# Down projection of a ConvFFN layer: the latent tokens as seven block products of 512 tokens, 1408 features and 512 columns, the context tile beside them

## The chip, the cores and the metric

The kernel runs on one core of a Trainium2 chip, in float32 with each operand split into a high part that the matmul takes exactly (float32r) and a low remainder. The metric is the device time of one execution in microseconds (us).

## The reference, cut to what matters

One trunk layer of a hybrid diffusion backbone. 128 context tokens and 1024 latent tokens (1152 in all, 9 tiles of 128) share the weights; only the gates (`gt2`) differ. The last steps are what the change touches:

```
up = dwconv_rows(h2 @ w_up, conv_w, conv_b);  ug, uv = split(up)
f  = (gelu(ug) * uv) @ w_down            # (1152 x 2816) @ (2816 x 1024)
x  = x + gt2 * rmsnorm(f, g_post_ffn)    # root mean square over all 1024 columns
```

## The kernel before, in words

The features (2816 = 22 tiles of 128) come out of the up projection transposed, features on partitions, and go to a DRAM scratch `f_dram`. The up projection itself already runs as seven block products per feature tile pair; ScalarE (ACT) makes the high parts, VectorE (DVE) the low parts and the sums out of PSUM, GpSimd (POOL) the sums of weight blocks (`weight_sum`, L902) and the product of gate and value (L915).

The down projection follows it. Its work is cut into 66 cells (`down_cell`): for each of three rounds r of 384 tokens, 22 feature tiles k. A cell needs 128 x 1024 weights and 128 x 384 features. They are loaded by SyncE (SP) into one of four slots (`down_load`, `f_load`; a cell's load waits until the cell four earlier is ready), ACT copies both to their high parts (`down_split` in ACT, L1822 and L1824), DVE subtracts to get the low parts (`down_split` in DVE, `sub_hi`, L1927) and signals `down_ready`. TensorE (PE) then runs 18 matmuls of 512 columns (3 token tiles x 2 column halves x 3 products high*high, high*low, low*high; L1326). PE's `down_used` or `done2` frees the slot for ACT.

A round's three tiles of 1024 columns are in three of four pairs of PSUM banks. After its last cell, ACT squares each tile out of PSUM with a running sum (`final_stats`), DVE makes mean, reciprocal root and the product with the gate row into `yo` (`finish`, L2508), POOL adds the residual `x1ld` (L941) and issues the stores and the next loads of the residual. The last tile is finished by DVE alone and stored by SP and ACT, half by half; the last four cells run tile by tile (`down_end`).

The order on each engine is written out by hand; all waits are semaphores. In the last unit of the up projection (s = NP-1), `next_weights` puts the splits of cells 0 to 2 among the taps and sums of that unit on ACT and DVE; cell 3's split comes after the unit's last gelu and taps.

Of the kernel before, what the change touches and what calls it, by code (L numbers as in the profile page):

```python
# [27 lines left out]
P = 128  # L28
# [79 lines left out]
def build(nc, x_prompt, x_sample, state_C, state_n, state_m, c, c_ctx, w_ada, b_ada, g_pre_mix, g_post_mix,  # L108
# [197 lines left out]
    for n, name in enumerate(quarters):  # L306
# [26 lines left out]
    down_at = [R + 32 * HT + 16 * n * HT for n in range(DR)]  # L333
    down_hi = [place(f"down_hi{n}", [P, 1024], F32R, at=at) for n, at in enumerate(down_at)]
    down_lo = [place(f"down_lo{n}", [P, 1024], F32R, at=at + 4096) for n, at in enumerate(down_at)]
    down_raw = [place(f"down_raw{n}", [P, 1024], at=at + 4096 * h)
                for n, (at, h) in enumerate((raw_at[(NP + b) % 2], h) for b in range(2) for h in range(2))]
    f_hi = [place(f"f_hi{n}", [P, BW], F32R, at=HH0 + 4 * T * n) for n in range(DR)]
    f_lo = [place(f"f_lo{n}", [P, BW], F32R, at=HH0 + 32 * T + 4 * T * n) for n in range(DR)]
    g_at = [LD0 + 8192 + 4 * T] + [HH0 + 4 * T * (4 + n) for n in range(1, DR)]  # L340
    f_raw = [place(f"f_raw{n}", [P, BW], at=at) for n, at in enumerate(g_at)]
    x1ld = place("x1ld", [P, 4, DM], at=R)
    yo = place("yo", [P, 3, DM], at=R + 96 * HT)
    y_junk = place("y_junk", [P, DM], at=R + 96 * HT + 12288)
# [19 lines left out]
    plain_g_dram = nc.dram_tensor("z_plain_g", (PLAIN, P, T), F32, kind="Internal").ap()  # L364
    f_dram = nc.dram_tensor("z_f", (NF, P, T), F32, kind="Internal").ap()
# [66 lines left out]
    x1_in = [S(f"x1_in{i}") for i in range(4)]  # L432
    last_done = S("last_done")
    y_stored = [S("y_stored0"), S("y_stored1"), S("y_stored2")]
    y_last = [S("y_last0"), S("y_last1")]
# [29 lines left out]

    def put_out(eng, t):

        if t < NT - 1:
            eng.wait_ge(final_done, t + 1)
        else:  # L470
            eng.wait_ge(last_done, 1)
            eng.dma_start(y_sample[0, (t - 1) * P:t * P, 0:512], yo[:, t % 3, 0:512]).then_inc(y_last[1], 16)
            return
        dst = y_prompt[0] if t == 0 else y_sample[0, (t - 1) * P:t * P, :]
        eng.dma_start(dst, yo[:, t % 3, :]).then_inc(y_stored[t % 3] if t < NT - 2 else y_last[t - NT + 2], 16)

# [55 lines left out]

    def down_cell(n):
        return n % NF, n // NF

    def down_slot_free(eng, n):

        k, r = down_cell(n - DR)
        if k == NF - 1:
            eng.wait_ge(done2, NT + TB * (r + 1))  # L540
        else:
            eng.wait_ge(down_used, n - DR - r + 1)
# [56 lines left out]
    with nc.Block() as block:  # L599

        @block.sync
        def _(sp):
# [108 lines left out]
            def down_load(n):  # L711

                k, r = down_cell(n)
                if n < DR:
                    sp.wait_ge(up_lo_done, 7 * (NP - 1 + n // 2))
                else:
                    sp.wait_ge(down_ready, n - DR + 1)
                sp.dma_start(down_raw[n % DR][:, :], w_down[0][k * P:(k + 1) * P, :]).then_inc(down_in[n % DR], 16)

            def f_load(n):  # L720

                k, r = down_cell(n)
                if n == 0:
                    sp.wait_ge(plain_stored, 16 * 3 * PLAIN)
                elif n < DR:
                    sp.wait_ge(product_done, 7 * (NP - 1) + 2)
                if r == 0 and k >= PLAIN:
                    for half in range(2):
                        sp.wait_ge(half_stored[half], 16 * (k - PLAIN + 1))
                sp.dma_start(f_raw[n % DR][:, :], f_dram[k][:, r * BW:(r + 1) * BW]).then_inc(f_in[n % DR], 16)  # L730
# [8 lines left out]
            for s in range(NP):  # L739
                if s + 2 < NP:  # L740
                    sp.wait_ge(up_lo_done, 7 * (s + 1))
                    up_load(s + 2)
                elif s == NP - 2:
                    down_load(0)
                    down_load(1)
                    f_load(0)
                else:
                    down_load(2)
                    down_load(3)
# [7 lines left out]
                if s == NP - 1:  # L757
                    for n in range(1, DR):
                        f_load(n)
            for n in (DR, DR + 1):  # L760
                down_load(n)
                f_load(n)
            half_store(NP - 1, 0)
            half_store(NP - 1, 1)
            for n in range(DR + 2, NB * NF):
                down_load(n)
                f_load(n)
            put_out(sp, NT - 2)
            put_out(sp, NT - 1)

            for d in range(3):
                sp.wait_ge(y_stored[d], 16 * ((NT - d) // 3))
            sp.wait_ge(y_last[0], 16)
            sp.wait_ge(y_last[1], 32)
# [5 lines left out]
        def _(pool):  # L780
# [154 lines left out]
            pool.wait_ge(product_done, 7 * (NP - 1) + 5)  # L935
            for t in range(4):
                pool.dma_start(x1ld[:, t % 4, :], x1_dram[t]).then_inc(x1_in[t % 4], 16)
            for t in range(NT - 1):
                pool.wait_ge(evac2, NT + t + 1)
                pool.wait_ge(x1_in[t % 4], 16 * (t // 4 + 1))  # L940
                pool.tensor_tensor(yo[:, t % 3, :], yo[:, t % 3, :], x1ld[:, t % 4, :], ALU.add).then_inc(final_done, 1)  # L941
                if t < NT - 2:
                    put_out(pool, t)
                if t + 4 < NT:
                    pool.wait_ge(final_done, t + 1)
                    pool.dma_start(x1ld[:, t % 4, :], x1_dram[t + 4]).then_inc(x1_in[t % 4], 16)


        @block.tensor
        def _(pe):  # L950
# [362 lines left out]
            def down_tile(n, j, halves=(0, 1)):  # L1313

                k, r = down_cell(n)
                q = TB * r + j
                bank = SLOT_BANK[(7 * NP + q) % 4]
                if k == 0 and halves[0] == 0:
                    if q >= 4:
                        pe.wait_ge(evac2, NT + q - 3)  # L1320
                    else:
                        product_freed(pe, 7 * NP - 4 + q)
                tok = slice(j * P, (j + 1) * P)
                for x, w, first, last in ((f_hi, down_hi, True, False), (f_hi, down_lo, False, False), (f_lo, down_hi, False, True)):
                    for hb in halves:
                        mm = pe.matmul(ps[:, bank + hb, :], x[n % DR][:, tok], w[n % DR][:, hb * 512:(hb + 1) * 512],  # L1326
                                       start=(k == 0 and first), stop=(k == NF - 1 and last))
                return mm

            def down_feature(n):  # L1330

                k, r = down_cell(n)
                pe.wait_ge(down_ready, n + 1)
                for j in range(TB):
                    mm = down_tile(n, j)
                    if k == NF - 1:
                        mm.then_inc(done2, 1)
                if k < NF - 1:
                    mm.then_inc(down_used, 1)

            def down_end():

                for j in range(TB - 1):
                    for n in range(NB * NF - DR, NB * NF):
                        if j == 0:
                            pe.wait_ge(down_ready, n + 1)
                        mm = down_tile(n, j)
                    mm.then_inc(done2, 1)
                for n in range(NB * NF - DR, NB * NF):
                    mm = down_tile(n, TB - 1, (0,))  # L1350
                mm.then_inc(done1, 1)
                for n in range(NB * NF - DR, NB * NF):
                    mm = down_tile(n, TB - 1, (1,))
# [32 lines left out]
            for n in range(NB * NF - DR):  # L1386
                down_feature(n)
# [4 lines left out]
        def _(act):  # L1392
# [420 lines left out]
            def down_split(n):  # L1813

                k, r = down_cell(n)
                d = n % DR
                act.wait_ge(down_in[d], 16 * (n // DR + 1))
# [4 lines left out]
                act.activation(down_hi[d][:, :], down_raw[d][:, :], ACT.Copy)  # L1822
                act.wait_ge(f_in[d], 16 * (n // DR + 1))
                act.activation(f_hi[d][:, :], f_raw[d][:, :], ACT.Copy).then_inc(down_hi_done, 1)  # L1824

            def next_weights(s, i):
# [3 lines left out]
                elif i in (2, 3, 4):  # L1830
                    down_split(i - 2)
# [50 lines left out]
            def final_stats(q):  # L1882

                bank = SLOT_BANK[(7 * NP + q) % 4]
                if q == NT - 1:

                    act.wait_ge(done1, 3 * KD + NB * PLAIN + 1)
                    act.wait_ge(final_roots, 2 * q)
                    act.activation(y_junk[:, 0:512], ps[:, bank, :], ACT.Square, accum_out=hstat[:, 0, q:q + 1]).then_inc(final_roots, 1)
# [657 lines left out]
```

## Time and profile before

| what | us |
|---|---|
| median of 3 runs (1790.91 to 1791.72) | 1791.66 |
| the profiled execution | 1790.54 |
| its span, first to last instruction | 1788.7 |
| PE busy, DVE busy, ACT busy, POOL busy in the span | 1771.9, 1128.6, 672.3, 283.2 |
| down projection: first to last start of its matmuls | 1508.1 to 1778.6 |
| its 1188 matmuls, mean duration of one | 0.39 |

The profile's page gives, for one execution, each engine's busy time, the busy share in slices of the span, the DMA queues, the chain that ended last, and groups of like instructions with their mean duration and the wait ahead of them. A matmul's duration overlaps the next one's: the pace is read from starts. The mean granted TensorE clock is 0.998 of full speed.

### The profile page before, as it was taken

What the parts mean: (1) busy time and instruction counts of PE and PEld (TensorE: products, weight loads), DVE (VectorE), ACT (ScalarE), POOL (GpSimd) and SP (SyncE); (2) the same over time, 40 slices, a digit from 0 to 9 for tenths busy, and PEclk for the clock granted to TensorE, in tenths of its full rate; (3) what the DMA queues carried; (4) which work ended last, traced back from release to release, by engine and by line L of the source; (5) the groups of instructions that cost most, each with busy time, mean ns of one, the idle gap of its engine ahead of it and who ended that gap; (6) DMA issues with size and microseconds to landing.
All of it is one profiled execution on the core that took longest, in us unless ns stands there. A gap on an engine that the chain in (4) does not pass through costs nothing.

```text
span 1788.7 us, 26788 instructions
## 1 busy us (share of the span) xinstructions
PE 1771.9 (99%) x10627; PEld 1659.0 (93%) x10627; DVE 1128.6 (63%) x2330; ACT 672.3 (38%) x1132; POOL 283.2 (16%) x278
## 2 busy tenths in 40 slices
PE   9999999999999999999999999999999999999997
PEld 3999999999999999999988999999999999888886
DVE  4786566565566544463555688888888888454543
ACT  3723212333134243451344544443444444343432
POOL 1010000100000100010010252444333333020101
PEclk9999999999999999999999999999999999999999
DMA  9133334424433544373332322333222223757562
GB/s 349 51 98 113 93 102 128 126 76 152 105 115 126 148 116 143 131 253 110 97 123 86 112 95 81 107 113 99 84 75 71 81 79 115 271 185 241 182 225 76
DMA packets 200720, 229.66 MB, mean 128 GB/s; under 512 B 9840, under 2 KB 163324, under 8 KB 200596
## 3 DMA queue, kind: packets, MB, share of 16 engines
q1 hardware_dynamic: 183060, 164.66, 30.3%
q0 software_dynamic: 13056, 46.39, 7.5%
q10 hardware_dynamic: 4480, 16.91, 2.3%
q8 instruction: 84, 1.38, 0.3%
q14 instruction: 40, 0.33, 0.1%
HBM read 180.77 MB, written 47.15 MB: 127 GB/s over the span
## 4 chain that ended last, share of the span: by engine, by line
PE 91%; DVE 5%; SPq 1%; ACT 1%; issue 1%; DMA 1%; DVEq 0%; ACTq 0%
PE ps L1298 22%; PE ps L1326 14%; PE ps L958 12%; PE ps L960 12%; PE ps L959 12%; PE ps L1240 5%; PE ps L1123 2%; PE ps L1124 2%; PE ps L1125 2%; PE ps L1107 2%; PE ps L1111 2%; PE ps L1109 2%; DVE ada_part L2146 1%; DVE H_lo L1927 1%; PE ps L987 1%
## 5 line engine op out<-in xcount | busy, mean ns | idle before, releaser
L958 PE MATMUL ps<-H_hi,ring_hi 128*128 128x384 f32 x1224 | 422.6, 345 | 0.9 <-DVE H_lo L1927 0.4
L959 PE MATMUL ps<-H_lo,ring_hi 128*128 128x384 f32 x1224 | 409.5, 335 | 0.0
L960 PE MATMUL ps<-H_hi,ring_lo 128*128 128x384 f32 x1224 | 409.5, 335 | 0.0
L958 PEld LDWEIGHTS ps<-H_hi,ring_hi 128*128 128x128 f32 x1224 | 229.9, 188 | 4.2 <-DVE H_lo L1927 2.1
L959 PEld LDWEIGHTS ps<-H_lo,ring_hi 128*128 128x128 f32 x1224 | 230.1, 188 | 1.0
L960 PEld LDWEIGHTS ps<-H_hi,ring_lo 128*128 128x128 f32 x1224 | 229.8, 188 | 0.0
L1927 DVE TENSOR_TENSOR down_lo<-down_raw,down_hi 128x1024 fp32r<-128x1024 f32 x66 | 86.0, 1303 | 122.9 <-ACT f_hi L1824 122.6
L2110 DVE SCALAR_TENSOR_TENSOR Cst<-Cst,GE,ps 128x257 f32<-128x257 f32 x56 | 27.0, 483 | 165.4 <-PE ps L1111 165.4
L1298 PE MATMUL ps<-T_hi,up_hi 128*128 128x288 f32 x608 | 130.5, 296 | 0.4 <-ACT held_g L1803 0.3
L1298 PE MATMUL ps<-T_hi,up_lo 128*128 128x288 f32 x608 | 130.2, 296 | 0.0
L1298 PE MATMUL ps<-T_lo,up_hi 128*128 128x288 f32 x608 | 130.1, 296 | 0.0
L1927 DVE TENSOR_TENSOR up_lo<-up_raw,up_hi 128x512 fp32r<-128x512 f32 x114 | 88.4, 779 | 57.5 <-ACT up_hi L1761 57.5
L1326 PE MATMUL ps<-down_hi,f_hi 128*128 128x512 f32 x396 | 122.9, 390 | 0.5 <-DVE yo L2508 0.5
L1326 PE MATMUL ps<-down_lo,f_hi 128*128 128x512 f32 x396 | 122.6, 389 | 0.0
L1326 PE MATMUL ps<-down_hi,f_lo 128*128 128x512 f32 x396 | 122.6, 389 | 0.0
L1822 ACT ACTIVATE down_hi<-down_raw 128x1024 fp32r<-128x1024 f32 x66 | 69.9, 1059 | 140.2 <-PE ps L1326 125.2
L2146 DVE SCALAR_TENSOR_TENSOR ada_part<-raw,condT,ada_part 128x128 f32<-128x128 f32 x448 | 120.3, 346 | 0.0
L1927 DVE TENSOR_TENSOR ring_lo<-raw,ring_hi 128x1024 fp32r<-128x1024 f32 (+1 forms) x69 | 82.4, 1198 | 33.1 <-ACT ring_hi L1410 30.2
L1298 PEld LDWEIGHTS ps<-T_hi,up_hi 128*128 128x128 f32 x608 | 97.8, 189 | 1.3 <-ACT held_g L1803 0.9
L561 ACT ACTIVATE stage<-ps 128x384 f32<-128x384 f32 x72 | 35.2, 488 | 168.5 <-PE ps L960 168.5
L1298 PEld LDWEIGHTS ps<-T_lo,up_hi 128*128 128x128 f32 x608 | 97.9, 189 | 0.0
L1298 PEld LDWEIGHTS ps<-T_hi,up_lo 128*128 128x128 f32 x608 | 97.9, 189 | 0.0
(298 smaller groups left out, 3578.2 us busy)
## 6 DMA issues: line engine op xcount, KB each, us to landing
down_raw<-in_w_down_dram SPq DMA_DIRECT2D x66, 512.0 KB, 3.7
raw<-in_w_in_dram SPq DMA_DIRECT2D x44, 512.0 KB, 4.1
up_raw<-in_w_up_dram SPq DMA_DIRECT2D x38, 512.0 KB, 5.2
raw<-in_w_ada_dram SPq DMA_DIRECT2D x32, 512.0 KB, 5.4
f_raw<-z_f SPq DMA_DIRECT2D x66, 192.0 KB, 3.8
GE<-z_gates SPq DMA_DIRECT2D x72, 128.0 KB, 4.1
z_f<-mid_v SPq DMA_DIRECT2D x19, 288.0 KB, 5.2
z_f<-mid_g SPq DMA_DIRECT2D x19, 288.0 KB, 2.1
```

The costliest lines, as they stand in the source:

```text
L958: pe.matmul(out, whi, xhi, start=first, stop=False)
L959: pe.matmul(out, whi, xlo, start=False, stop=False)
L960: return pe.matmul(out, wlo, xhi, start=False, stop=last)
L1107: pe.matmul(ps[:, 5 + d, 0:VW], Pt[:, d, :], vaug[v][:, cx, :], start=True, stop=(i == 0))
L1109: mm = pe.matmul(ps[:, 5 + d, 0:VW], qs[:, d, :], Cst[:, d, :], start=False, stop=True)
L1111: mm = pe.matmul(ps[:, 7, 0:VW], k_weighted[:, d, :], vaug[v][:, cx, :], start=True, stop=True)
L1240: mm = pe.matmul(ps[:, bank + hb, :], x[:, k, tok], w[:, hb * 512:(hb + 1) * 512], start=(n == 0 and first), stop=(n == KD - 1 and last))
L1298: mm = pe.matmul(ps[:, bank + sb, 0:SB], wt[:, w], x[:, k0 + k, cols], start=(k == 0 and n == 0), stop=(k == KD // 2 - 1 and n == 2))
L1326: mm = pe.matmul(ps[:, bank + hb, :], x[n % DR][:, tok], w[n % DR][:, hb * 512:(hb + 1) * 512], start=(k == 0 and first), stop=(k == NF - ...
L1822: act.activation(down_hi[d][:, :], down_raw[d][:, :], ACT.Copy)
L1927: return dve.tensor_tensor(out, full, hi.bitcast(F32), ALU.subtract)
L2146: ins = dve.scalar_tensor_tensor(out=part, in0=w, scalar=condT[:, cond, k:k + 1], in1=part, op0=ALU.mult, op1=ALU.add)
```

## The change

The three rounds are replaced by seven products over the latent tokens. With X11, X12 the two feature halves (11 tiles each) of the first 512 latent tokens, X21, X22 those of the second 512, and W11 to W22 the quarters of `w_down` (1408 features x 512 columns), the products are formed from sums and differences of blocks on both sides, and the four result quarters (`c11`, `c12`, `c21`, `c22`, in SBUF) from sums of products. A cell is now one feature tile of one product: 77 cells, n = 11 p + j. PE runs 12 matmuls in a cell (4 token tiles x 3), and 15 in products 0, 2 and 6, in which the context tile's 128 tokens go along (`down_context`). The context's last block, kept back in `fk_hi`, `fk_lo`, `W12_hi`, `W12_lo`, runs after everything else (33 matmuls). PSUM: products alternate between two sets of four banks.

What each engine does per cell after: SP loads a 128 x 512 weight block, in products 1, 3, 4 and 5 a second one; POOL subtracts the two there (and stores the difference in products 3 and 4, to be read in 4 and 5); ACT copies weight and feature tile to high parts (128 x 512 each, 128 x 128 more with the context); DVE subtracts for the low parts, and makes the feature combination (`combine`) in products 1 to 4. At a product's end ACT (product 0) or DVE (`product_sums`) takes the four banks out of PSUM. Statistics are taken by halves; POOL adds the residual and issues a store for each 128 x 512 half tile of the latent tokens.

The diff, cut to what sets the order and the work:

```diff
 # ---- SP
+                if n >= DR:
                     sp.wait_ge(down_ready, n - DR + 1)
+                    if (n - DR) // NC in (3, 4):
+                        m = diff_no(n - DR) - NC
+                        sp.wait_ge(w_diff_stored[m % 2], 16 * (m // 2 + 1))
...
+                sp.dma_start(w_raw[d][:, :], first).then_inc(down_in[d], 16)
+                if p in DIFF:
...
+                    sp.dma_start(w_sub[d][:, :], second).then_inc(down_in[d], 16)
...
                 elif s == NP - 2:
-                    down_load(0)
-                    down_load(1)
-                    f_load(0)
+                    for n in range(DR):
+                        w_load(n)
...
                 if s == NP - 1:
-                    for n in range(1, DR):
+                    for n in range(DR):
                         f_load(n)
...
+                if n == 6 * NC + DR - 1:
+                    for i in range(4):
+                        x1_load(i)
+            sp.wait_ge(down_ready, CELLS)
+            for i in range(4, NT):
+                x1_load(i)
 # ---- POOL
-                pool.tensor_tensor(yo[:, t % 3, :], yo[:, t % 3, :], x1ld[:, t % 4, :], ALU.add).then_inc(final_done, 1)
+            for p in DIFF:
+                for j in range(NC):
...
+                    pool.tensor_tensor(w_raw[d][:, :], w_raw[d][:, :], w_sub[d][:, :], ALU.subtract).then_inc(weight_sums, 1)
+                    if p in (3, 4):
...
+                        pool.dma_start(w_diff_dram[p - 3][j], w_raw[d][:, :]).then_inc(w_diff_stored[m % 2], 16)
+            for i, t in enumerate(X1_ORDER[:NT - 1]):
+                pool.wait_ge(x1_in[i % 3], 16 * (i // 3 + 1))
+                for h in range(2):
+                    c = slice(512 * h, 512 * (h + 1))
+                    pool.wait_ge(last_done, 2 * i + h + 1)
+                    pool.tensor_tensor(half_tile(t, h), half_tile(t, h), x1t[t][:, c], ALU.add).then_inc(final_done, 1)
+                    pool.wait_ge(final_done, 2 * i + h + 1)
+                    pool.dma_start(y_sample[0, (t - 1) * P:t * P, c], half_tile(t, h)).then_inc(y_stored, 16)
 # ---- PE
+                if j == 0:
+                    product_freed(pe, 7 * NP - 2) if p == 0 else pe.wait_ge(evac2, summed_at[p - 1, 0])
...
+                tail = range(CELLS - TAIL_CELLS, CELLS)
+                for t in TILE_ORDER:
+                    for n in tail:
+                        if t == TILE_ORDER[0]:
                             pe.wait_ge(down_ready, n + 1)
+                        mm = down_tile(n, t)
                     mm.then_inc(done2, 1)
+                for n in tail:
+                    down_context(n)
+                pe.wait_ge(evac2, summed_at[6, TILE_ORDER[0]])
+                for j in range(NC):
+                    mm = down_mm(SET[1][0], fk_hi[j][:, :], fk_lo[j][:, :], W12_hi[j][:, :], W12_lo[j][:, :], False, j == NC - 1)
 # ---- ACT
+                act.activation(B_hi[d][:, :], w_raw[d][:, :], ACT.Copy)
+                if p in (0, 2) or cell_inputs(n):
+                    act.wait_ge(f_in[d], f_count(n))
+                if p in (1, 3, 4, 6):
+                    act.wait_ge(combined, NC * {1: 0, 3: 1, 4: 2, 6: 3}[p] + j + 1)
...
+                ins = act.activation(A_hi[d][:, :], src[:, :], ACT.Copy)
...
-                elif i in (2, 3, 4):
-                    down_split(i - 2)
+                elif i in (3, 4, 5):
+                    down_split(i - 3)
...
+            for n in range(3, CELLS):
+                if n == last_cell(0) + DR:
+                    first_copies()
+                if n == last_cell(2) + DR + 2:
+                    for t in (1, 2, 3, 4, 0):
+                        half_squares(t)
...
+                if n == last_cell(5) + DR + 4:
+                    for t in (5, 6, 7, 8):
+                        root(t)
                 down_split(n)
 # ---- DVE
+                if n + 1 < CELLS and (n + 1) // NC == 1:
+                    combine(n + 1)
+                if p in (2, 3, 4):
+                    combine(n)
                 dve.wait_ge(down_hi_done, n + 1)
+                sub_hi(B_lo[d][:, :], w_raw[d][:, :], B_hi[d][:, :])
...
+                ins = sub_hi(A_lo[d][:, :], src[:, :], A_hi[d][:, :])
...
+                    elif p == 3:
+                        steps = ((c22, c21, ALU.add), (c12, c12, ALU.add))
+                    elif p == 4:
+                        steps = ((c21, c21, ALU.add), (c22, c22, ALU.add), (c12, c12, ALU.add))
...
+                    for out, x, op in steps:
+                        ins = dve.tensor_tensor(out[:, t, :], x[:, t, :], q, op)
...
+            for n in range(3, CELLS):
+                for p in range(1, 6):
+                    if n == last_cell(p) + DR:
+                        product_sums(p)
...
+                if n == last_cell(5) + DR + 5:
+                    for t in (5, 6, 7, 8):
+                        gated(t)
                 down_split(n)
+            product_sums(6)
+            for t in LAST_TILES:
+                mean(t)
+                gated(t)
```

`gated(t)` takes a reciprocal and two in-place products of a half tile in SBUF with the gate row in SBUF (128 x 512 each).

## Rows read from the trace of the kernel before

**Rows 1.** The chain that ended last, from 1480 us: start, us, what.
```profile
1479.87 28.38 PE ps L1298 x213
1508.25 85.70 PE ps L1326 x378
...
1691.65 87.35 PE ps L1326 x384
```
**Rows 2.** Engines' busy time in the down projection: stretch, us, busy and instructions.
```profile
1508.00:1778.70 270.70, 270.17 (x1190) 222.62 (x1189) 136.83 (x162) 107.25 (x156) 30.84 (x26) 1.00 0.58 194
```
**Rows 3.** DVE's timeline in the middle of a round: start, us, engine, line, operation.
```profile
1641.39 1.23 DVE L1927 TENSOR_TENSOR down_lo<-down_raw,down_hi 128x1024 fp32r<-128x1024 f32 x1 [2.39 <-ACT f_hi L1824]
...
1645.47 1.23 DVE L1927 TENSOR_TENSOR down_lo<-down_raw,down_hi 128x1024 fp32r<-128x1024 f32 x1 [2.39 <-ACT f_hi L1824]
```
**Rows 4.** Groups of one tile or line: duration ns min/median/max, first and last start.
```profile
L1927 DVE TENSOR_TENSOR up_lo<-up_raw,up_hi x114: 678/686/1782, 1067.0 to 1492.4; 128x512 fp32r<-128x512 f32 x114
L902 POOL TENSOR_TENSOR up_raw<-up_raw x38: 1287/1296/1698, 1056.8 to 1483.5; 128x512 f32<-128x512 f32 x38
L941 POOL TENSOR_TENSOR yo<-yo,x1ld x8: 2382/2406/2415, 1599.6 to 1776.7; 128x1024 f32<-128x1024 f32 x8
L2485 DVE TENSOR_TENSOR yo<-ps,gtb x2: 683/686/690, 1777.1 to 1779.9; 128x512 f32<-128x512 f32 x2
```
**Rows 5.** Timeline of DVE, ACT and POOL in the up projection's seven-product stage.
```profile
1400.22 0.75 DVE L2387 TENSOR_TENSOR held_v<-held_v,ps 128x576 f32<-128x576 f32 x1
1400.48 1.30 POOL L902 TENSOR_TENSOR up_s<-up_raw 128x512 f32<-128x512 f32 x1 [4.30 <-DVE up_lo L1927]
1401.08 0.76 DVE L2387 TENSOR_TENSOR held_g<-held_g,ps 128x576 f32<-128x576 f32 x1
...
1403.74 0.69 DVE L1927 TENSOR_TENSOR up_lo<-up_raw,up_hi 128x512 fp32r<-128x512 f32 x1
1403.97 1.74 POOL L915 TENSOR_TENSOR mid_v<-mid_g,mid_v 128x576 f32<-128x576 f32 x1 [2.20 <-DVE mid_v L2401]
1404.34 2.82 DVE L2401 SCALAR_TENSOR_TENSOR mid_g<-held_g,vT,mid_g 128x567 f32<-128x567 f32 x2
```
**Rows 6.** Timeline after the first round: PE's gap, DVE's subtraction, POOL's add and issue.
```profile
1599.59 0.73 PE L1326 MATMUL ps<-down_hi,f_hi 128*128 128x512 f32 x2 [0.21 <-DVE yo L2508]
...
1603.08 3.86 DVE L1927 TENSOR_TENSOR down_lo<-down_raw,down_hi 128x1024 fp32r<-128x1024 f32 x1
1603.43 2.42 POOL L941 TENSOR_TENSOR yo<-yo,x1ld 128x1024 f32<-128x1024 f32 x1
1606.15 0.58 POOL L475 DMA_DIRECT2D out_dram<-yo  x1 [0.30 <-POOL yo L941]
```
**Rows 7.** Timelines of ACT, SP and DVE where the down projection begins.
```profile
1482.71 0.68 DVE L1927 TENSOR_TENSOR up_lo<-up_raw,up_hi 128x512 fp32r<-128x512 f32 x1
1483.31 0.75 DVE L2387 TENSOR_TENSOR held_v<-held_g,ps 128x576 f32<-128x576 f32 x1
...
1486.59 0.62 ACT L1761 ACTIVATE up_hi<-up_raw 128x512 fp32r<-128x512 f32 x1
...
1499.07 1.41 SPq L730 DMA_DIRECT2D f_raw<-z_f  x3
...
1501.63 0.53 ACT L1824 ACTIVATE f_hi<-f_raw 128x384 fp32r<-128x384 f32 x1 [1.42 <-DMA f_raw<-z_f]
...
1509.36 0.75 DVE L2387 TENSOR_TENSOR held_v<-held_v,ps 128x576 f32<-128x576 f32 x1
...
1517.77 1.23 DVE L1927 TENSOR_TENSOR down_lo<-down_raw,down_hi 128x1024 fp32r<-128x1024 f32 x1 [2.19 <-ACT f_hi L1824]
```
**Rows 8.** DMA issues from 1500 us to the end: KB each, median us to landing.
```profile
down_raw<-in_w_down_dram SPq DMA_DIRECT2D x62, 512.0 KB, 3.7
f_raw<-z_f SPq DMA_DIRECT2D x64, 192.0 KB, 3.8
```
**Rows 9.** DMA issues from 1514 to 1530 us, and the engines' row of 1515 to 1530 (last two columns: DMA share, GB/s).
```profile
down_raw<-in_w_down_dram SPq DMA_DIRECT2D x5, 512.0 KB, 10.4
...
1515.00:1530.00 15.00, 15.00 (x68) 12.43 (x67) 7.18 (x9) 6.48 (x10) 3.55 (x5) 1.00 0.80 299
```
**Rows 10.** The end: PE's last piece of the chain, then ACT's square and last store.
```profile
1775.81 3.19 PE ps L1326 x14
...
1779.02 0.60 ACT L1891 ACTIVATE y_junk<-ps 128x512 f32<-128x512 f32 x1 [2.03 <-PE ps L1326]
1779.51 0.19 ACT L1891 ACTIVATION_READ_ACCUMULATOR y_junk<-ps 128x1 f32 x1
...
1782.13 0.34 ACTq L1896 DMA_DIRECT2D out_dram<-yo  x1
```

More of the change, by code:

```diff
@@ L339, in build @@
[L339 to L344, printed above, removed]
+    h_piece = lambda g, k, half: HH0 + 32 * T * g + 4 * T * k + 4 * HT * half
+    X11 = [place(f"X11_{j}", [P, 512], at=h_piece(j // KD, j % KD, 0)) for j in range(NC)]
@@ new lines, in f_count, with w_count, diff_no, w_diff_count @@
+    def f_count(n):
+        return 16 * sum(cell_inputs(m) for m in range(n % DR, n + 1, DR))
+    def w_count(n):
+        return 16 * sum(2 if m // NC in DIFF else 1 for m in range(n % DR, n + 1, DR))
+    def diff_no(n):
+        p, j = down_cell(n)
+        return NC * DIFF[p] + j
+    def w_diff_count(n):
+        return 4 * NP + diff_no(n) + 1
+    done_at, at = {}, NT
+    for p in range(7):
+        for t in TILE_ORDER:
+            at += 1
+            done_at[p, t] = at
+        if p in (0, 2):
+            at += 1
+            done_at[p, "c"] = at
@@ new lines, in build @@
+    done_at[6, "c"] = at + 1
+    summed_at, at = {}, NT
+    for p in range(1, 7):
+        for t in TILE_ORDER + (("c",) if p == 2 else ()):
+            at += 1
+            summed_at[p, t] = at
+    last_cell = lambda p: NC * (p + 1) - 1
+    LAST_TILES = tuple(t + 1 for t in TILE_ORDER)
+    stat_of, root_of, mean_of = {}, {}, {}
+    for n, (what, t) in enumerate([("half", t) for t in (1, 2, 3, 4, 0, 5, 6, 7, 8)] + [("rest", t) for t in (5, 6, 7, 8)]
+                                  + [("root", t) for t in (5, 6, 7, 8)]
+                                  + [(what, t) for t in LAST_TILES + (0,) for what in ("rest", "root")]):
+        (root_of if what == "root" else stat_of)[what, t] = n + 1
@@ L536, in down_slot_free, with half_tile @@
+    for n, (what, t) in enumerate([("half", t) for t in (1, 2, 3, 4, 0, 5, 6, 7, 8)] + [("rest", t) for t in (5, 6, 7, 8)]
+                                  + [("rest", t) for t in LAST_TILES + (0,)]):
+        mean_of[what, t] = n + 1
+    X1_ORDER = (5, 6, 7, 8) + LAST_TILES + (0,)
+    def half_tile(t, h):
+        if t == 0:
+            return c0[h][:, :]
+        return ((c11, c12) if t < 5 else (c21, c22))[h][:, (t - 1) % 4, :]
     def down_slot_free(eng, n):
-        k, r = down_cell(n - DR)
@@ L727, in f_load @@
-                if r == 0 and k >= PLAIN:
+                elif n == NC:
+                    sp.wait_ge(product_done, 7 * NP)
+                if (p == 0 and k >= PLAIN) or p == 2:
                     for half in range(2):
                         sp.wait_ge(half_stored[half], 16 * (k - PLAIN + 1))
-                sp.dma_start(f_raw[n % DR][:, :], f_dram[k][:, r * BW:(r + 1) * BW]).then_inc(f_in[n % DR], 16)
+                elif n == NC:
+                    for half in range(2):
+                        sp.wait_ge(half_stored[half], 16 * NP)
@@ L1311, in up_pair @@
                 product(s, 6, H_hi, H_lo, KD // 2, HT)
[L1313 to L1328, printed above, removed]
@@ new lines, in sum_squares, with half_squares @@
+            def sum_squares(what, t, src, sums):
+                n = stat_of[what, t]
+                if n > 1:
+                    act.wait_ge(final_roots, n - 1)
+                act.activation(y_junk[:, :], src, ACT.Square, accum_out=sums[:, 0, t:t + 1]).then_inc(final_roots, 1)
+            def half_squares(t):
+                act.wait_ge(evac2, summed_at[2, "c" if t == 0 else t - 1] if t < 5 else summed_at[4, t - 5])
+                sum_squares("half", t, half_tile(t, 0 if t < 5 else 1), hstat)
```

410 lines of the change are left out of this document (261 added, 149 removed).

## The prediction

> **What bounds the kernel now.** I read the chain that ended last first: from 1480 us it is PE alone but for short pieces between rounds [rows 1], so the down projection is bound by matmuls. Then the busy times there: PE 270.2 of 270.7 us, DVE 136.8, ACT 107.3, POOL 30.8 [rows 2]. Then the pace: DVE's splits of one cell begin 4.08 us apart, each after a wait of 2.4 us [rows 3], which is 18 matmuls at 0.2267 us. Last, pairs of overlapping instructions on DVE and POOL, because the change gives both more work per matmul.
>
> **What PE saves.** Before: 66 x 18 = 1188 matmuls. After: 77 x 12 = 924 for the latent tokens, and 4 x 33 = 132 for the context, 1056 in all. 132 x 0.2267 = 29.9 us. If every edit had cover, the span would be about 1759.
>
> **What DVE and POOL do to each other.** A POOL subtraction of 128x512 takes 1.29 us, DVE's 0.686 [rows 4]; in a row DVE starts one 0.60 after another (1482.71 to 1483.31 [rows 7]). When both inputs of the DVE instruction are in SBUF, the two take turns: a low-part subtraction of 1.23 us took 3.86 while POOL added for 2.42 [rows 6]; POOL's product at 1403.97 took 1.74 behind a DVE subtraction, and the DVE pair after it 2.82 [rows 5]. When one DVE input is in PSUM, neither is longer (0.75 and 0.76 beside 1.30 [rows 5]). So a POOL subtraction costs up to 1.29 us of DVE's time, except under PSUM sums and while DVE waits anyway. Before, eight adds lay in 270 us; now there are 44 subtractions and 16 half adds.
>
> **Cell by cell.** PE needs 12 x 0.2267 = 2.72 us for a cell, 3.40 with the context. DVE needs:
> - Products 0 and 6: two low parts and a 128-column one, 1.5 us (2.1 with W12's): covered.
> - Product 1: combination and two low parts 1.83, POOL 1.29, so 3.12. It loses 0.4 a cell over seven cells after the boundary; the lead there is about 4 us (three ready cells, 8.2, less ACT's last copy 0.6, two ACT copies 1.2, low parts 1.3, POOL 1.3). Hidden.
> - Product 2: 2.1 of 3.4, no POOL but at its end. Hidden.
> - Products 3 and 4: DVE combines (0.69), waits for ACT's copy of the result (0.62 [rows 7] and the semaphores), then subtracts twice (1.25): 2.6 us in series, and nothing of it overlaps the cell before, since `combine(n)` is issued only just ahead of its own wait. POOL adds between 0.65 (it fits into DVE's wait) and 1.29. Weights land about 4 us after their issue [rows 8], the wait falls at no fixed phase of that, so I take 0.85: 3.45 a cell against 2.72.
> - Product 5: 1.22 + 1.29 = 2.5. Just covered.
>
> **The middle.** From the end of product 2 to the start of product 5's fourth cell PE needs 25 cells x 2.72 = 68.0 us. DVE, which has nothing beyond three ready cells, needs: five sums of product 2, 3.1 (0.62 each, from 0.686 [rows 4]); 19 cells x 3.45 = 65.5; five means and one product 1.2; the wait for ACT's five squares (0.6 + 0.19 each [rows 10]), of which about 2.0 is not hidden; eight sums of product 3, 5.0; three cells of product 5, 7.5; twelve sums of product 4, 7.4; one more split, 1.3. Sum 93.0; POOL gets about four subtractions done under the PSUM sums, -5.0: 88. **PE stalls 20 us.** Bounds: with no turns taken at all 73.3 us, a stall of 5; with every POOL subtraction added in full 101.6, a stall of 34.
>
> **The start.** Features of cell 0 are now loaded only after the half store at 1498.7, where three loads went before at 1499.07, and ACT waited until 1501.63 for one of them [rows 7]. Now it is two per cell, and ACT's and DVE's split of cell 0 stands ahead of the last unit's sums; PE's context matmuls wait for the sum that ran at 1509.36. That sum comes some 3 us later, and cell 3 (1517.77 + 1.6 before [rows 7]) at about 1521.5, where PE's three cells last 10.2 us instead of 12.2. I take 3.5 us; bounds 1 (only the shorter cells) and 6.
>
> **Transfers.** Products 1, 3 and 4 move 768 KB in 2.72 us, 289 GB/s, against 172 before. A stretch of 15 us at 299 GB/s had the DMA engines busy 0.80 [rows 9], so it fits, and the ring gives 10.9 us for load (5), POOL (1.3), two copies (1.2) and low parts (1.3). Cost 0 to 10, taken as 0. In product 6 SP issues four residual loads of 512 KB in a row and stops at the fourth until the first has landed; when such four were under way before, weights took 10.4 us [rows 9]. With ACT's four squares, roots and table load I take 3 us for products 5 and 6 (0 to 8).
>
> **The tail.** Before cell 74, DVE gates four tiles (8 instructions of 0.65, both inputs in SBUF), and POOL follows with 8 adds of 1.29 with 0.3 + 0.58 for wait and DMA issue between them [rows 6]. DVE starts this about 4.2 us after cell 69's matmuls end, and its work to cell 76's readiness is 5.2 + 0.8 (reciprocals) + 5.5 (splits), with all of POOL's 10.3 between: 4.2 + 21 = 25 us. PE is there after four cells and two thirds of a tile, 15 us, since the tile order asks for cell 76 almost at once. Stall 9.5; bounds 1 (no turns) and 15 (PE has no lead by then).
> From T, when cell 76 is ready, PE has 72 matmuls, 16.3 us, and the context's own end, as long as that from 1779.0 to 1788.7, 9.7 us: T + 26. But POOL ends later. The sums are done at T + 7.5, the first half is gated at T + 9, and eight POOL steps of 2.3 follow, the last add ending at T + 26.4; from the issue of the last store to the end it took 6.6 us [rows 10], and a POOL-issued store a little more: **T + 33.5**, 7.5 behind the context.
>
> **Sum.** Start 1508.2; 984 matmuls up to T, 223.1; stalls 3.5 + 20 + 3 + 9.5 = 36: T = 1767.3. Span 1800.8. The profiled execution was 1.8 over its span, 1802.6; the median of the runs is 1.1 above it: **1803.7**, 12 us or 0.7% slower. The seven products save 30 us of matmuls, and about 42 come back.
>
> The granted clock is 1.00 in the down projection [rows 2], whose gaps on PE are like the 0.21 us ahead of 1599.59 [rows 6], so no row shows it after 9 us of idling. The Trainium skill (TensorE: Matmul & The Clock Gate, What's actually happening) says that an engine that has been idle falls to half rate until it is busy again. By it the four tiles after T would come at half pace, at most 6.8 us later, and POOL's chain with them: about 1810. No run here shows it yet.
>
> **Rivals.**
> - *The cover holds, faster.* One mechanism: POOL's 128x512 work falls into DVE's waits and PSUM sums instead of between subtractions, and decides from the point where a product-3 cell takes DVE under 2.72 us. Then the middle stalls 5, the tail 1, the rest 4.5: T = 1741.8, and with POOL's own end, which stays, a span of 1775.3, **1778**. For it: DVE has a wait of 0.65 per cell and 15 us of PSUM sums, 28 us of room for 28 us of subtractions. Against it: nothing aligns them. Chance 0.27; between it and the forecast, 1788 to 1795, 0.11.
> - *Forecast*, DVE bound in products 3 and 4 and POOL last: 1795 to 1814, 0.47.
> - *Transfers are late as well.* At the 194 GB/s that the stage moved on average [rows 2], 768 KB would take 4.0 us: 33 cells lose 1.2, 41 us in place of the middle's 20: 1825. Speaks for it the ring of only four cells; against, the 299 GB/s. Chance 0.08, and 0.07 for the clock (1810).
>
> **Numbers.** A difference under 0.2% (3.6 us) is about what a measurement of this kernel can't tell from none. Faster 0.28, same 0.10, slower 0.62. Range 1775 to 1817; the likeliest case alone 1795 to 1814.
>
> **What would show it.** PE waiting for DVE (A_lo) in products 3 and 4, about 0.7 us a cell; DVE's subtractions above 0.69 on average there; a PE gap of some 10 us before cell 76; POOL's add and store as the last work, several us after PE's end. It is wrong if products 3 to 5 run at 2.72 us a cell.

## The result, and the profile after

The changed kernel takes 1803.94 us (median of 4 runs, 1802.34 to 1806.74) against 1791.58: a ratio of 1.0071, 95% interval 1.0054 to 1.0089, so 0.7% slower. The forecast was 1803.7. Its profiled execution has a span of 1800.5 us.

The chain that ended last, from the page (shares of the span by engine), had been PE 91% and DVE 5%. Now DVE and POOL stand in it:

```profile
PE 68%; DVE 17%; POOL 4%; issue 4%; ACT 4%; DMA 2%; SPq 1%; DVEq 0%; POOLq 0%; ACTq 0%
```

Busy time by stretch (us; PE, PEld, DVE, ACT, POOL, granted clock, DMA share, GB/s) answers to [rows 2]. The down projection and the places where PE stood still: its start, the sums after products 3 and 4, the wait for cell 76:

```profile
1508.00:1518.00 10.00, 7.52 (x27) 5.81 (x27) 9.71 (x17) 3.84 (x6) 1.47 (x1) 0.83 0.34 106
1649.00:1667.00 18.00, 14.09 (x52) 10.91 (x51) 18.00 (x27) 5.76 (x10) 9.46 (x10) 0.83 0.70 234
1686.00:1702.00 16.00, 13.33 (x53) 10.51 (x52) 12.32 (x21) 8.43 (x18) 6.45 (x6) 0.89 0.43 148
1748.00:1763.00 15.00, 4.70 (x13) 2.52 (x11) 14.96 (x16) 0.00 (x0) 9.36 (x11) 0.67 0.27 105
...
1508.00:1781.00 273.00, 252.04 (x1059) 203.53 (x1058) 219.95 (x324) 117.53 (x243) 106.19 (x91) 0.95 0.65 219
```

In three of them DVE has hardly an idle moment and PE has, and the granted clock falls behind each gap. The groups of like instructions (count | busy us, mean ns | wait before) show who gets longer, against medians of 0.686 and 1.296 us before [rows 4]:

```profile
L1049 POOL TENSOR_TENSOR w_raw<-w_raw,w_sub 128x512 f32<-128x512 f32 x44 | 69.6, 1583 | 99.0 <-DMA w_sub<-in_w_down_dram 90.5 <-DMA w_sub<-z_w_diff 8.3
L2103 DVE TENSOR_TENSOR B_lo<-w_raw,B_hi 128x512 fp32r<-128x512 f32 x77 | 67.3, 874 | 45.4 <-ACT fc_hi L1976 18.2 <-ACT A_hi L1972 16.0 <-ACT fk_hi L1976 11.1
L2103 DVE TENSOR_TENSOR A_lo<-X,A_hi 128x512 fp32r<-128x512 f32 x77 | 63.8, 828 | 0.0
...
L2723 DVE SCALAR_TENSOR_TENSOR c<-c,stat,gtb 128x512 f32<-128x512 f32 x16 | 23.6, 1515 | 0.3
L2702 DVE TENSOR_TENSOR c<-c,ps 128x512 f32<-128x512 f32 x36 | 22.3, 681 | 6.3 <-PE ps L1434 6.3
```

The sums out of PSUM (L2702) keep their 0.68; the means of the groups with two inputs in SBUF are longer. The medians are not (0.69 for the low parts): in the stages with POOL's 44 subtractions, 28 DVE instructions took 1.2 to 2.25 us and the others what they take alone. The 28 come to 28 us more, and POOL's 44 to 13 us more than 1.29 each.

DVE's two bursts of sums, after products 3 and 4, begin shortly before PE's two gaps in the middle (1657.7 and 1694.5):

```profile
1654.18 4.86 DVE L2702 TENSOR_TENSOR c<-c,ps 128x512 f32<-128x512 f32 x8
...
1689.03 7.26 DVE L2702 TENSOR_TENSOR c<-c,ps 128x512 f32<-128x512 f32 x12
```

All terms of the sum. The losses are the distances between the first matmuls of successive cells, less 2.72 or 3.40 us; T is the end of cell 76's split (1762.9):

| term of the sum | forecast | measured |
|---|---|---|
| cells 0 and 1 | 3.5 | 4.4 |
| products 3 to 5 | 20 | 13.6 |
| other boundaries of products, loads | 3 | 1.2 |
| wait for cell 76 | 9.5 | 12.4 |
| T | 1767.3 | 1762.9 |
| from T to the end | 33.5 | 37.6 |
| span | 1800.8 | 1800.5 |

That the total is right to 0.3 us is luck: T came 4.4 us earlier than forecast, and the rest took 4.1 us more. Within T, 6.4 us too much for the middle and 1.8 for the loads stand against 3.8 too little for the start and for cell 76.

### The profile page after: what moved, and what is told of

Same layout as the page of the kernel before. It is cut to its first block, busy times and chain, and to the rows that moved or that the text cites. A ratio compares the mean times of both kernels' runs of the same rounds, so it can differ in the third digit from the quotient of the medians.

```text
span 1800.5 us, 27040 instructions
## 1 busy us (share of the span) xinstructions
PE 1752.6 (97%) x10495; PEld 1639.4 (91%) x10495; DVE 1216.9 (68%) x2493; ACT 680.4 (38%) x1219; POOL 367.6 (20%) x352
## 4 chain that ended last, share of the span: by engine, by line
PE 68%; DVE 17%; POOL 4%; issue 4%; ACT 4%; DMA 2%; SPq 1%; DVEq 0%; POOLq 0%; ACTq 0%
PE ps L1075 12%; PE ps L1077 12%; PE ps L1076 12%; PE ps L1415 8%; PE ps L1357 5%; DVE mid_g L2577 3%; DVE up_lo L2103 3%; DVE mid_v L2577 2%; PE ps L1432 2%; PE ps L1240 2%; PE ps L1433 2%; PE ps L1434 2%; PE ps L1241 2%; PE ps L1242 2%; POOL w_raw L1049 2%
## 5 line engine op out<-in xcount | busy, mean ns | idle before, releaser
L1432 PE MATMUL ps<-B_hi,A_hi 128*128 128x512 f32 x308 | 124.8, 405 | 17.9 <-DVE fc_lo L2103 10.3
L1433 PE MATMUL ps<-B_lo,A_hi 128*128 128x512 f32 x308 | 123.3, 400 | 0.0
L1434 PE MATMUL ps<-B_hi,A_lo 128*128 128x512 f32 x308 | 122.9, 399 | 0.0
L2103 DVE TENSOR_TENSOR B_lo<-w_raw,B_hi 128x512 fp32r<-128x512 f32 x77 | 67.3, 874 | 45.4 <-ACT fc_hi L1976 18.2
L1415 PE MATMUL ps<-H_hi,up_lo 128*128 128x288 f32 x456 | 97.8, 296 | 0.0
```

The lines of the kernel that those rows point to most:

```text
L1415: mm = pe.matmul(ps[:, bank + sb, 0:SB], wt[:, w], x[:, k0 + k, cols], start=(k == 0 and n == 0), stop=(k == KD // 2 - 1 and n == 2))
L1432: pe.matmul(out, xhi, whi, start=first, stop=False)
L1433: pe.matmul(out, xhi, wlo, start=False, stop=False)
L1434: return pe.matmul(out, xlo, whi, start=False, stop=last)
L2103: return dve.tensor_tensor(out, full, hi.bitcast(F32), ALU.subtract)
```

## Experiments

Theory A: DVE instructions with two inputs in SBUF and POOL's 128x512 operations take turns, and that is what PE waits for. Rivals: DVE's bursts of sums (B), the lower clock (C), the transfers (D). "Before" had 1790.6 to 1791.2 us beside these runs.

**e1, the subtraction on POOL left out.**
```diff
-                    pool.tensor_tensor(w_raw[d][:, :], w_raw[d][:, :], w_sub[d][:, :], ALU.subtract).then_inc(weight_sums, 1)
```


> The 44 weight subtractions on GpSimd are left out (the loads and the stores of the blocks stay, so the products use unsubtracted weights). Theory A, VectorE and GpSimd take turns at SBUF: the PE waits in products 3 to 5 (13.6 us, some 4 of them from the lower clock that followed) shrink to 2 or less, VectorE's low-part subtractions there all take 0.69, the gap before cell 76 stays about 12; time 1790 to 1793. Rival B, VectorE's own bursts of 8 and 12 sums are what PE waits for: the waits after products 3 and 4 stay 8 us or more, time 1798 to 1802. Rival D, the transfers are late: nothing changes, 1803.


ACT waits for the load in its place. Measured 1789.5 us (ratio to before 0.9989, 0.9979 to 0.9998). PE lost 1.0 us in products 3 to 5 in place of 13.6, with all bursts of sums and all loads still there. Busy times of the stretch of products 3 to 5 (columns as above), where POOL has nothing but the issues of stores:
```profile
1618.00:1706.00 88.00, 87.59 (x385) 71.94 (x384) 67.73 (x119) 44.84 (x87) 9.18 (x17) 1.00 0.75 244
```
At 244 GB/s and with the bursts PE runs through: B and D fall as causes by themselves. The wait for cell 76 stayed at 12. What e1 can't separate is the turns from the time that ACT waits for POOL's result, as both went.

**e12, a memset in its place.** 128x512 on POOL as before, but only written.
```diff
-                    pool.tensor_tensor(w_raw[d][:, :], w_raw[d][:, :], w_sub[d][:, :], ALU.subtract).then_inc(weight_sums, 1)
+                    pool.memset(w_sub[d][:, :], 0.0).then_inc(weight_sums, 1)
```


> The GpSimd subtraction is replaced by a memset of the second block (128x512, GpSimd only writes; the products use unsubtracted weights). If what is shared is the way in which the second input is read, VectorE's low parts in products 1, 3, 4, 5 take 0.69 as with nothing there, PE's waits stay under 2 us in products 3 to 5 and the time is that of e1, 1790. If any GpSimd access holds VectorE up: means of 0.8 or more and waits of 5 us or more.


A single run: 1789.57 us, 0.9 us lost in products 3 to 5. POOL's line (duration ns min/median/max):
```profile
L1049 POOL MEMSET w_sub<- x44: 525/527/531, 1536.8 to 1697.4; 128x512 f32 x44
```
36 of the 44 overlap a DVE instruction, and no DVE instruction of 128x512 beside them is over 0.8 us: the mean of the low parts is 0.709 and 0.703 as in e1 (0.710, 0.704). So POOL writing does not hold DVE up. ACT waits for POOL here as in the changed kernel, though for 0.53 us of work and not 1.29; a read-free instruction of 1.29 us was not tried.

**e5, the subtraction on DVE**, one cell ahead; the stores stay on POOL.
```diff
-                    pool.tensor_tensor(w_raw[d][:, :], w_raw[d][:, :], w_sub[d][:, :], ALU.subtract).then_inc(weight_sums, 1)
+                if n + 1 < CELLS and (n + 1) // NC in DIFF:    # in DVE's down_split(n)
+                    e = (n + 1) % DR
+                    dve.wait_ge(down_in[e], w_count(n + 1))
+                    dve.tensor_tensor(w_raw[e][:, :], w_raw[e][:, :], w_sub[e][:, :], ALU.subtract).then_inc(weight_sums, 1)
```


> The 44 weight subtractions move from GpSimd to VectorE, one cell ahead; the stores of the differences stay on GpSimd. Theory A (turns at SBUF): a subtraction beside VectorE's work cost it 1.1 us and kept GpSimd waiting up to 4.5 us, on VectorE it costs 0.6 in order; the waits of PE in products 3 to 5 go from 13.6 to 2 to 5 us, the gap before cell 76 stays 12; 1792 to 1796. Rival (VectorE has too much work of any kind): 0.6 us more per cell on VectorE makes it no better, 1803 or more.


Measured 1798.29 us (1.0045, 1.0030 to 1.0060), slower than forecast: products 3 to 5 lose 8.3, not 2 to 5. All 44 subtractions took 0.68 to 0.70 us there, so no turns were taken, and yet two stops of PE stay behind the bursts, 2.0 and 2.2 us. DVE needs 2.4 us for a cell now instead of 1.8 and has less to spare against PE's 2.72; 3.4 of the 8.3 is matmuls at the lower clock. So B is no cause alone, but a partner: DVE's bursts hurt once its work per cell comes near PE's 2.72. The start was worse too (5.9 for 4.4), which no theory here explains.

**e11, only the bursts spread**, one token tile a cell over four cells (the squares and means that follow product 4's sums come two cells later for it).
```diff
+                    if p in (3, 4):
+                        if 0 <= n - last_cell(p) - DR < 4:
+                            product_sums(p, TILE_ORDER[n - last_cell(p) - DR:][:1])
```


> The changed kernel with only the sums of products 3 and 4 spread over four cells each, GpSimd's subtractions kept. If the bursts alone make the 13.6 us of waits in products 3 to 5, they go to 3 or less and the time to 1792. If bursts and turns add up to more than VectorE has, about half stays: waits 4 to 9 us, 1796 to 1800.


Measured 1801.24 us (1.0061, 1.0045 to 1.0078); products 3 to 5 still lose 11.6, where 4 to 9 were expected. With POOL's subtractions in place, how the sums are laid out hardly matters. Bursts and turns make the 13.6 us together: without the turns 1.0 is left (e1), with the turns and without bursts 11.6.

**e2, gates of tiles 5 to 8 behind the last split** (order only: the loop over `gated` moves from before cell 74's split to after `product_sums(6)`).
```diff
-                if n == last_cell(5) + DR + 5:
-                    for t in (5, 6, 7, 8):
-                        gated(t)
                 down_split(n)
             product_sums(6)
+            for t in (5, 6, 7, 8):
+                gated(t)
```


> Order only: the gating of the four tiles 5 to 8 goes behind the last split and product 6's sums. A: no gap before cell 76 (PE gets there at about 1750.5 and not 1762.9), clock stays at full there, but GpSimd then has 16 adds in a row of about 2.2 us after the sums, so the end comes about T + 45 to 50: 1797 to 1803, no gain in time. Rival (cells 74 to 76 are late for their loads or ScalarE): the gap stays 8 us or more.


Measured 1805.36 us (1.0076, 1.0061 to 1.0091), above the 1797 to 1803 expected. The gap is gone, the clock is full there, and the end comes 36 us after PE's last matmul:
```profile
1745.00:1766.00 21.00, 21.00 (x94) 17.40 (x93) 14.53 (x20) 2.08 (x5) 6.43 (x7) 1.00 0.41 150
1766.00:1800.00 34.00, 0.46 (x2) 0.02 (x1) 27.15 (x25) 3.87 (x13) 24.01 (x26) 0.58 0.32 124
```
PE's last matmul came 15 us sooner and the end 2 us later: the 16 adds and gates, in a row, are the path here.

**e4, the adds left out** (no residual in the latent output).
```diff
-                    pool.tensor_tensor(half_tile(t, h), half_tile(t, h), x1t[t][:, c], ALU.add).then_inc(final_done, 1)
-                    pool.wait_ge(final_done, 2 * i + h + 1)
```


> The 16 residual adds on GpSimd are left out (the residual is missing from the latent output; gates and stores stay). A: gates take 0.67 to 0.75 each, the gap before cell 76 goes to 1 us or less, the clock doesn't fall there, and the end is bound by the context's matmuls again, T + 26 to 28: 1779 to 1783. Rival B (VectorE's own eight gates and the tile-by-tile tail are too much): the gap stays 5 us or more, time 1788 or more.


Measured 1782.01 us (0.9950, 0.9933 to 0.9966). Each gate takes what it takes alone, the stores still being issued by POOL:
```profile
L2721 DVE SCALAR_TENSOR_TENSOR c<-c,stat,gtb x16: 743/749/753, 1740.0 to 1766.4; 128x512 f32<-128x512 f32 x16
```
The wait for cell 76 is 0.9 us, and the end comes 25 us after T. Products 3 to 5 lose 14.1 as before. With the adds, the kernel takes 22 us more.

**e3, stores issued by SP** and not between POOL's adds.
```diff
-                    pool.wait_ge(final_done, 2 * i + h + 1)
-                    pool.dma_start(y_sample[0, (t - 1) * P:t * P, c], half_tile(t, h)).then_inc(y_stored, 16)
+                    sp.wait_ge(final_done, 2 * i + h + 1)    # in a loop at SP's end
+                    sp.dma_start(y_sample[0, (t - 1) * P:t * P, c], half_tile(t, h)).then_inc(y_stored, 16)
```


> The 16 output stores of the latent tokens are issued by SyncE at its end and not by GpSimd between its adds. If the DMA issue on GpSimd holds VectorE up as the add does (VectorE's gated halves took 2.2 us, 0.4 more than beside a subtraction alone), a step falls from 2.16 to about 1.95 in the gap before cell 76 and after it: gap 10 to 11 and the end some 2 to 3 us nearer to T, 1799 to 1801. If the issue only uses GpSimd's own time and VectorE is slowed by the add alone: VectorE's gates fall to 1.8, the same sum. If neither: 1804.


Measured 1793.83 us (1.0012, 1.0003 to 1.0022), a gain of 10 us where 3 to 5 were expected: T comes 3.6 us sooner, and the end 30.1 after T and not 37.6. Of these 7.5 us, 5.4 are gone by the end of POOL's last add and 2.1 behind it. POOL's adds run without a break, and DVE's gates fit between them one for one (POOL's line, then DVE's):
```profile
1742.69 8.50 POOL L1067 TENSOR_TENSOR c<-c,x1t 128x512 f32<-128x512 f32 x5
```
```profile
1745.09 3.29 DVE L2726 SCALAR_TENSOR_TENSOR c<-c,stat,gtb 128x512 f32<-128x512 f32 x2
```
That is 1.65 us a gate. In the changed kernel it was 2.1, and DVE's instruction began inside POOL's DMA issue, ahead of the add:
```profile
1745.89 4.21 DVE L2723 SCALAR_TENSOR_TENSOR c<-c,stat,gtb 128x512 f32<-128x512 f32 x2
...
1754.29 2.21 DVE L2103 TENSOR_TENSOR B_lo<-w_raw,B_hi 128x512 fp32r<-128x512 f32 x1
1756.42 2.21 DVE L2103 TENSOR_TENSOR A_lo<-X,A_hi 128x512 fp32r<-128x512 f32 x1
```
```profile
1754.10 0.55 POOL L1064 DMA_DIRECT2D out_dram<-c  x1 [0.30 <-POOL c L1062]
1754.67 1.27 POOL L1062 TENSOR_TENSOR c<-c,x1t 128x512 f32<-128x512 f32 x1
1756.24 0.55 POOL L1064 DMA_DIRECT2D out_dram<-c  x1 [0.30 <-POOL c L1062]
```
DVE's 1754.29 has nothing beside it but the issue for 0.4 us and still ends 0.56 after the add at 1754.67. In e5, where POOL issues stores with no such operation behind them, DVE's subtractions keep 0.69. So the issue alone doesn't hold DVE; an add that stands right behind it seems to do so already then. That is read from these three kernels; which part of POOL takes the turn was not measured.

**e7, PE kept busy in its gap** with 44 matmuls into a free bank.
```diff
+                pe.wait_ge(evac2, summed_at[5, TILE_ORDER[-1]])
+                for m in range(44):
+                    pe.matmul(ps[:, SET[1][1], :], fk_hi[0][:, :], W12_hi[0][:, :], start=True, stop=True)
```


> Added: 44 matmuls of 512 columns (10 us at 0.227) into a free PSUM bank between cell 73 and the wait for cell 74, where PE stood for 10 us and the granted clock fell for 13.7 us. Theory C (the lower clock costs time of its own): matmuls run 0.227 and not 0.427 from cell 76 on, the tiles' sums come 1.7 to 2 us sooner after cell 76 is ready, and the time is 1801 to 1802.5. Rival: GpSimd's chain sets the end and absorbs that, 1804. T itself stays at 1762.9.


Measured 1803.60 us (1.0070, 1.0053 to 1.0086): no gain. The clock is full in the stretch of the gap (the last but two columns), where it was 0.64 in the changed kernel:
```profile
1749.00:1763.00 14.00, 13.43 (x59) 10.81 (x58) 13.96 (x13) 0.51 (x2) 9.85 (x12) 1.00 0.29 112
```
T was 1764.7, as the wait behind product 4's sums was 4.7 us in this execution and not 2.8 (no run here says why), and from T to the end it took 37.5 again. The clock in the tail costs nothing, as the end goes by gates and adds. This run can't price the clock elsewhere: there, the cells behind the gaps (1, 47 and 58) lose 1.3, 2.6 and 1.7 us in the changed kernel, nearly all of it in matmuls 0.43 apart for 0.23: 5.6 us together.

**e6, features first:** the loads of cells 0 to 3 go ahead of the two half stores.
```diff
+                if s == NP - 1:
+                    for n in range(DR):
+                        f_load(n)
                 if s:
                     half_store(s - 1, 0)
                     half_store(s - 1, 1)
```


> Order on SyncE only: the feature loads of cells 0 to 3 go ahead of the two half stores of the last up unit but one. If cell 0's split on ScalarE and VectorE waits for its features and holds the sum that PE's first context matmul waits for, the 4.4 us lost in cells 0 and 1 (3.0 of waiting and 1.4 of the lower clock behind it) fall to 1 to 2 and the time to 1800 to 1802. If VectorE's splits are simply more work ahead of that sum, nothing changes: 1804.


Measured 1798.96 us (1.0043, 1.0028 to 1.0058). The start loses 0.1 us in place of 4.4, where 1 to 2 were expected to stay:
```profile
1508.00:1518.00 10.00, 10.00 (x48) 8.43 (x48) 7.68 (x12) 4.38 (x8) 3.29 (x2) 1.00 0.19 68
```

**e9, all of it on DVE.** e5 and e6, and: the differences are stored by ACT's queue, outputs by SP, and the adds go away. A half is multiplied by the gate row as soon as its squares are taken, and scale and residual are one instruction.
```diff
-                    pool.tensor_tensor(half_tile(t, h), half_tile(t, h), x1t[t][:, c], ALU.add).then_inc(final_done, 1)
+                dve.tensor_tensor(half_tile(t, h), half_tile(t, h), gtb2[:, 1, 512 * h:512 * (h + 1)], ALU.mult)
...
+                    dve.scalar_tensor_tensor(out=half_tile(t, h), in0=half_tile(t, h), scalar=stat[:, 3, t:t + 1],
+                                             in1=x1t[t][:, 512 * h:512 * (h + 1)], op0=ALU.mult, op1=ALU.add).then_inc(last_done, 1)
```


> GpSimd does nothing in the down projection: VectorE subtracts the weights, multiplies by the gate row ahead of the statistics where it can and adds the residual in the same instruction as the scale; differences are stored by ScalarE's queue, outputs by SyncE's; features of the first cells are loaded early. A: waits of PE 2 to 5 us in all, no gap before cell 76, clock full, and PE's context matmuls with their 10 us end set the time: 1508.2 + 239.4 + 4 + 10 = 1762, with what lies around the span 1762 to 1769, faster than both kernels. Rival (the VectorE is overloaded without GpSimd): 1785 or more.


Measured 1766.28 us, ratio to before 0.9865 (0.9850 to 0.9879): 1.35% faster than before, 2.1% faster than the change. DVE does more instructions in less time than in the changed kernel (211.1 us for 220.0), and POOL 3.3 for 106.2:
```profile
1508.00:1760.00 252.00, 244.99 (x1062) 200.44 (x1061) 211.10 (x383) 115.70 (x240) 3.31 (x2) 0.99 0.72 236
```
The end comes 6 us after PE's last matmul. Products 4 and 5 still lose 8.8 us (7.8 in e5). The two kernels differ in several things at once, so this run shows what they are worth together and not each by itself.

**e10 and e13, e9 with the sums spread,** as in e11; e13 also moves eight gate products out of cells 64 to 67 (four to cells 70 and 71, four behind the last split). The diff is e13 against e10.
```diff
-                if n in (last_cell(4) + DR + 6, last_cell(4) + DR + 7):
+                if n in (last_cell(5) + DR + 1, last_cell(5) + DR + 2):
...
-                if n in (last_cell(5) + 1, last_cell(5) + 2):
-                    for t in ((1, 2), (3, 4))[n - last_cell(5) - 1]:
-                        gate_half(t, 0)
```


> e9 with the sums of products 3 and 4 taken one token tile per cell over four cells instead of all before one split. e9 still lost 3.9 us in product 4 and 4.9 in product 5, each a wait of 2.4 or 3.3 before the fourth cell and the lower clock behind it. If these are the bursts of 5 and 7.4 us against a lead of three cells: no PE gap over 0.5 us there, clock at full, time 8 to 9 us below e9: 1757 to 1759. If VectorE is short of time in sum: the gaps stay 3 us or more together, 1762 or more.

> e10 took 4.3 us out of products 4 and 5 and lost 6.2 at the start of product 6: PE's first context matmul there waits for VectorE's sum of product 5 (4.4 us), which stands behind eight gate products of cells 65 to 68. Here these are moved, four to cells 70 and 71, four behind the last split. If that is the cause, product 6 starts with about 1 us of waiting again, PE's end comes 5 to 7 us sooner and the time is 1759 to 1762. If the spread sums themselves put VectorE too late: the gap stays 4 us or more and the time 1765 to 1767.


e10: 1766.08 us, 0.9865 (0.9850 to 0.9880), no better than e9, and not the 1757 to 1759 expected: 4.3 us came out of products 4 and 5, where 4.5 stayed, and 6.2 went in at product 6, whose first context matmul waited for a sum behind the gate products. e13: 1764.16 us, 0.9854 (0.9837 to 0.9870); its profiled execution took 1763.0, and the 4.4 us gap is 1.0 (e10's stretch first, then e13's):
```profile
1705.00:1720.00 15.00, 10.62 (x38) 8.28 (x37) 13.11 (x25) 7.15 (x17) 0.00 (x0) 0.82 0.89 306
```
```profile
1705.00:1720.00 15.00, 13.97 (x62) 11.25 (x61) 11.77 (x22) 8.23 (x20) 0.00 (x0) 1.00 0.92 326
```
So the cause was right in the profile, but the time missed the 1759 to 1762 expected, and by the intervals e13 can't be told from e9.

## Why the prediction was right, step by step

- *Turns on SBUF*, the step on which the sum rests: right, and shown by e1, e4 and e12 and by the durations in e5. Without POOL's subtractions 12.6 of 13.6 us go, without its adds 22 us.
- *DVE's time per cell in products 3 and 4*: wrong in its working. I said that `combine(n)` and the wait for ACT's copy stand in series (2.6 us). They don't: the combination made in a cell is for the next product (ACT asks for one eleven cells back), and DVE ran a cell in 1.81 us when undisturbed, three starts 0.60 apart. Nor did every subtraction of POOL cost it time: 22 of them made 12 DVE instructions longer, 0.62 us for each of the 22, where 0.85 was taken. That makes about 2.4 us a cell and not 3.45, under PE's 2.72, so DVE did not bind cell by cell. The sign named for it, about 0.7 us a cell, did not show: 23 of the 33 cells of products 3 to 5 took 2.72 to 2.75 us, and 11.2 of the 13.6 us lie in two gaps and the cells behind them, after the bursts of sums. The term was 6.4 us too large, although it held nothing for the lower clock, which gave 4.3.
- *What a waiting POOL costs*: missed. I counted only DVE's loss. With the same 2.4 us of DVE's time per cell, e5 loses 8.3 us in products 3 to 5 and the changed kernel 13.6; the difference is about what the late POOL costs (an estimate from the two). Here POOL's subtraction took 5.79 us, beside an unbroken run of DVE's, and ACT, which needs its result, held up cell 42:
```profile
1632.60 5.79 POOL L1049 TENSOR_TENSOR w_raw<-w_raw,w_sub 128x512 f32<-128x512 f32 x1 [0.79 <-DMA w_sub<-in_w_down_dram]
```
```profile
1632.94 0.68 DVE L2597 TENSOR_TENSOR X<-X,X 128x512 f32<-128x512 f32 x1
...
1636.55 0.68 DVE L2597 TENSOR_TENSOR X<-X,X 128x512 f32<-128x512 f32 x1
1639.60 1.50 DVE L2103 TENSOR_TENSOR B_lo<-w_raw,B_hi 128x512 fp32r<-128x512 f32 x1 [2.37 <-ACT A_hi L1972]
```
- *The start*: right in cause (e6), 3.5 for 4.4; 1.3 of the 4.4 is the lower clock, which was not in the sum.
- *Transfers hidden*: right (e1).
- *The wait for cell 76*: right in place and cause (e2, e4); 9.5 for 12.4. Half of that is in the adding up: 5.2 + 0.8 + 5.5 and POOL's 10.3 are 21.8 and not 21, which gives 26 against PE's 15 and so 11. The rest: a step of gate, add and issue took 2.1 to 2.2 us.
- *POOL's chain after T*: right in kind (e2, e3, e4), 33.5 for 37.6. POOL's last add ended at T + 28.3 for T + 26.4. The mean's instruction, 128x1 but with two inputs in SBUF, took 1.25 us beside an add and 0.16 without one (four times):
```profile
1774.34 1.25 DVE L2716 SCALAR_TENSOR_TENSOR stat<-stat,hstat 128x1 f32<-128x1 f32 x1
```
The other 2.2 us came behind the last add. The sum took 7.1 us from there to the end and gave the store as the reason; it was 9.3. The stores were not the last thing: SP, which waits for them all, was through at 1795.4, and the end came at 1800.5 with the closing instruction of POOL's queue (duration ns, start):
```profile
L661 POOLq DRAIN  x1: 8815/8815/8815, 1791.5 to 1791.5; - x1
...
L661 SPq DRAIN  x1: 7/7/7, 1795.4 to 1795.4; - x1
```
- *The clock*: the Trainium skill's rule (TensorE: Matmul & The Clock Gate, What's actually happening) agrees with the trace in kind: the granted clock fell from 1.00 to 0.67 over the stretch with the 10 us gap. It fell as well behind shorter ones, to 0.63 behind 2.5 us without a matmul at the start, and to 0.66 behind 1.9 us in e5. The place was wrong: the rival put its cost after T, where it cost nothing (e7), and the 5.6 us that it did cost at the start and in the middle were in no term.
- *The faster rival* (the cover holds): its condition, a product-3 cell under 2.72 us of DVE's time, was met on average, and 10 of 22 subtractions did cost DVE nothing, but the time was not saved, as the bursts and a late POOL came on top. The middle lost 13.6 us where this rival had 5.

## What to carry to other kernels

Before giving GpSimd a two-input operation to relieve VectorE, look in the trace for one VectorE instruction with two SBUF inputs that overlaps it. Here 44 subtractions of 128x512 on GpSimd cost VectorE 28 us of its own time, and doing them itself would have cost it 26 (0.60 each): nothing was relieved, and a late GpSimd came on top. When matmuls are saved, recount every engine's work per cell against the shorter cell, the tail included, and look for whom a late engine holds up in turn. With GpSimd out, and the start, the gates and the stores rearranged as well, the kernel with fewer matmuls was 25 us faster than the one before (e9); some 3.7 of these are the closing instruction of GpSimd, which ended that much after the other engines in the kernel before.

## What the runs showed of the hardware that I had not expected

- Starvation goes both ways: GpSimd's subtraction waited 4.5 us behind eight VectorE instructions in a row, which let nothing in between.
- A VectorE instruction of one element per partition with two SBUF inputs took 1.25 us beside a GpSimd add, 0.16 without; each time it ended with the add.
- With a GpSimd DMA issue between two adds, VectorE got one instruction per 2.15 us; without it one per 1.65 (e3), while an issue with no add behind it cost VectorE nothing (e5).
- GpSimd writing 128x512 took 0.53 us and held no one up (e12).
- GpSimd's queue closes late: its last DRAIN ended 8.2 us after the last issue in the changed kernel, 7.0 us after the last add in e3, which issues no store on GpSimd, and 9.4 us after it in the kernel before. Where GpSimd's last work lies near the end, this sets the end; in e9, where it lies at 1517, it cost nothing.
